# Feed-forward of a hybrid encoder block: nine of eleven chunks with the weights as the stationary operand and the activations moving

## The reference, cut to what matters

```
def rms_norm(x, g):
    y = x * rsqrt(mean(x * x, -1) + 1e-6)
    return y * g
def swiglu(h, w_gate, w_up, w_down):
    return (silu(h @ w_gate) * (h @ w_up)) @ w_down
for l in range(2):
    x = x + 0.5 * swiglu(rms_norm(x, ffn1_norm[l]), ...)     # w_gate, w_up: 1024 x 2816
    x = x + concat([attention, pooling], -1) @ w_out[l]       # mixing, not touched but for banks
    x = x + 0.5 * swiglu(rms_norm(x, ffn2_norm[l]), ...)     # w_down: 2816 x 1024
```

## Time and profile before

| | us |
|---|---|
| median of three runs | 951.69 |
| the profiled execution | 951.97 |
| its span, first to last instruction | 949.9 |
| PE busy | 931.3 |
| PE weight loads (beside the products) | 760.5 |
| DVE busy | 551.5 |
| ACT busy | 499.7 |

### The profile page before, as it was taken

How to read it: one execution, slowest core, us unless ns; L and a number is a source line. 1 busy time by engine, 2 the same in 40 slices (tenths; PEclk the granted TensorE clock), 3 DMA queues, 4 the chain that set the end, 5 groups by cost and what they waited for, 6 DMA issues and landing times.

```text
span 949.9 us, 12733 instructions
## 1 busy us (share of the span) xinstructions
PE 931.3 (98%) x4299; PEld 760.5 (80%) x4299; DVE 551.5 (58%) x896; ACT 499.7 (53%) x821; POOL 44.6 (5%) x81
## 2 busy tenths in 40 slices
PE   8899999999999999999999999999999999999996
PEld 6688888877777888888888888888877888888885
DVE  4546465467755655645476545565686474554644
ACT  6545454456746554545465445454675374554542
POOL 1001010010001100100010000000100000000000
PEclk9999999999999999999999999999999999999999
DMA  7967868726235987675456656644534266465541
GB/s 240 251 202 165 230 175 288 257 90 232 104 110 143 273 183 234 158 222 180 133 189 210 220 182 246 213 157 164 175 139 146 74 237 209 172 210 188 168 142 45
DMA packets 123532, 174.66 MB, mean 184 GB/s; under 512 B 8384, under 2 KB 99696, under 8 KB 123248
## 3 DMA queue, kind: packets, MB, share of 16 engines
q1 hardware_dynamic: 117744, 165.70, 52.0%
q0 software_dynamic: 2848, 6.38, 5.5%
q10 hardware_dynamic: 2912, 2.22, 0.7%
HBM read 173.14 MB, written 4.19 MB: 187 GB/s over the span
## 4 chain that ended last, share of the span: by engine, by line
PE 92%; DVE 3%; ACT 2%; issue 2%; DMA 1%; SPq 0%; POOL 0%; POOLq 0%; DVEq 0%; ACTq 0%
PE ps L985 28%; PE ps L988 28%; PE ps L986 28%; PE ps L1082 2%; PE ps L995 1%; DVE w_lo L727 1%; PE ps L996 1%; PE ps L1195 1%; ACT xt_hi L487 1%; PE ps L1211 1%; PE ps L1223 1%; PE ps L1070 1%; DMA w_raw<-in_ffn_w_down_dram 1%; PE ps L1045 0%; DVE w_lo L718 0%
## 5 line engine op out<-in xcount | busy, mean ns | idle before, releaser
L985 PE MATMUL ps<-w_hi,xt_hi 128*128 128x512 f32 x856 | 342.1, 400 | 2.1 <-DVE xt_lo L741 1.1
L727 DVE SCALAR_TENSOR_TENSOR w_lo<-w_raw,gains,w_hi 128x512 fp32r<-128x512 f32 x416 | 285.1, 745 | 85.8 <-ACT w_hi L472 84.3
L986 PE MATMUL ps<-w_lo,xt_hi 128*128 128x512 f32 x856 | 334.3, 390 | 0.0
L988 PE MATMUL ps<-w_hi,xt_lo 128*128 128x512 f32 x856 | 329.5, 391 | 0.0
L472 ACT ACTIVATE w_hi<-w_raw,gains 128x512 fp32r<-128x512 f32 x408 | 260.7, 713 | 86.2 <-PE ps L988 81.5
L718 DVE TENSOR_TENSOR w_lo<-w_raw,w_hi 128x1024 fp32r<-128x1024 f32 x104 | 122.8, 1222 | 136.1 <-ACT w_hi L465 135.7
L985 PEld LDWEIGHTS ps<-w_hi,xt_hi 128*128 128x128 f32 x856 | 161.2, 188 | 40.3 <-issue 4.0
L988 PEld LDWEIGHTS ps<-w_hi,xt_lo 128*128 128x128 f32 x856 | 161.1, 188 | 34.8
L986 PEld LDWEIGHTS ps<-w_lo,xt_hi 128*128 128x128 f32 x856 | 161.4, 189 | 30.7
L465 ACT ACTIVATE w_hi<-w_raw 128x1024 fp32r<-128x1024 f32 x104 | 104.4, 1052 | 121.7 <-PE ps L988 114.4
L985 PE MATMUL ps<-w_hi,gt_hi 128*128 128x512 f32 x352 | 138.3, 393 | 3.3 <-DVE gt_lo L782 3.3
(11 more groups left out here) (84 smaller groups left out, 404.2 us busy)
## 6 DMA issues: line engine op xcount, KB each, us to landing
w_raw<-in_ffn_w_down_dram SPq DMA_DIRECT2D x88, 512.0 KB, 4.2
w_raw<-in_ffn_w_gate_dram SPq DMA_DIRECT2D x86, 512.0 KB, 4.0
w_raw<-in_ffn_w_up_dram SPq DMA_DIRECT2D x86, 512.0 KB, 5.1
w_raw<-in_w_in_dram SPq DMA_DIRECT2D x32, 512.0 KB, 4.8
w_raw<-in_w_out_dram SPq DMA_DIRECT2D x16, 512.0 KB, 5.3
bias_scratch<-in_rpb_dram POOLq DMA_DIRECT2D x32, 96.0 KB, 8.2
bias<-bias_scratch POOLq DMA_DIRECT2D x2, 1536.0 KB, 6.8
pool_m<-in_pool_matrix_dram ACTq DMA_DIRECT2D x1, 1024.0 KB, 9.3
```

The source lines that it names most:

```text
L727: nc.vector.scalar_tensor_tensor(w_lo[slot][:, part], w_raw[slot][:, part], g, w_hi[slot][:, part].bitcast(F32), ALU.mult, ALU.subtract).t ...
L985: nc.tensor.matmul(o, hi, wh, start=start, stop=False)
L986: nc.tensor.matmul(o, hi, wl, start=False, stop=False)
L988: last = nc.tensor.matmul(o, lo, wh, start=False, stop=bool(stop))
```

## The change

Chunks 0 and 1 of a stage stay as they were. For chunks 2 to 10 the operands of gate and up trade places. The stationary operand is now a 128x128 block of the weights, the moving operand is the normalised, transposed activation `xn`, 256 tokens at once. The output has hidden columns on partitions and tokens along the row, which is the form that the down product wants, so `gated` is not transposed any more. For one chunk there are 2 halves of rows, gate and up, 2 column blocks, 4 row blocks and 3 products: 96 products of 256 columns where there were 48 of 512. They go to banks 0, 1 (gate) and 6, 7 (up).

For that, each stage makes `xn` once while chunk 1 runs: PE spreads `rstd` over a row (`broadcast_rstd`), ACT stores it, DVE multiplies the transposed residual with gain and `rstd` (`normalise_xt`, 8 instructions of 256 columns), ACT and DVE split it (`split_xn_hi`, `split_xn_lo`). The transposed residual must stay in PSUM until then, so `transpose_resid` writes the accumulator banks now, and the first down product waits for `normed_t_ready`. The weights of chunks 2 to 10 are split without the gain, by 2 instructions of 1024 columns where there were 4 of 512. `silu` and `gate_t` work on 512 columns at once. The order of loads in SP's loop changes from g0, g1, d to g0, d, g1.

```diff
-                with sp.Fori(2, N_FF_CHUNKS) as i:
-                    load_gate_up(layer, ff, weights, i, 0)
-                    load_gate_up(layer, ff, weights, i, 1)
-                    load_down(layer, ff, weights, i - 1, ff["d"], i - 1)
+                with sp.Fori(2, LAST) as i:
+                    load_gate_up(layer, ff, weights, i + 1, 0)
+                    load_down(layer, ff, weights, i, ff["d"], i)
+                    load_gate_up(layer, ff, weights, i + 1, 1)
...
+            def silu_t_of(layer, ff, i):
+                act.wait_ge(gate_ready, transposed_no(layer, ff, i) + 1)
+                nc.scalar.activation(silu[:, :, :], ps[:, 0:2, 0:SEQ], ACT.Silu
+                                     ).then_inc(silu_t_ready, 1)
...
+            def gate_t(layer, ff, i, part):
+                dve.wait_ge(up_ready, transposed_no(layer, ff, i) + 1)
+                dve.wait_ge(silu_t_ready, transposed_no(layer, ff, i) + 1)
+                nc.vector.scalar_tensor_tensor(gated[:, :, part], ps[:, 6:8, part], 0.5,
+                                               silu[:, :, part], ALU.mult, ALU.mult
+                                               ).then_inc(gated_t_ready, 1)
...
+            def normalise_xt(layer, ff):
+                dve.wait_ge(rstd_row_stored, ff_no(layer, ff) + 1)
+                for k in range(KT):
+                    h, c = k // 4, (k % 4) * P
+                    done = nc.vector.scalar_tensor_tensor(
+                        normed_t(k).rearrange("p (t q) -> p t q", t=TT),
+                        ps[:, 2 + h:6 + h:2, c:c + P], gains[:, ff["stage"], layer, k:k + 1],
+                        rstd_row[:, :].rearrange("p (t q) -> p t q", t=TT), ALU.mult, ALU.mult)
+                    if k % 4 == 3:
+                        done.then_inc(normed_t_ready, 1)
...
-                        last = nc.tensor.transpose(ps[:, 6 + h, k * P:(k + 1) * P],
+                        last = nc.tensor.transpose(acc(t, h)[:, k * P:(k + 1) * P],
                                                    resid[:, t, c:c + P], ident[:, :])
...
+            def broadcast_rstd(layer, ff):
+                for t in range(TT):
+                    pe.wait_ge(rstd_ready[t], layer * STAGES + (ff["stage"] + 1))
+                    last = nc.tensor.matmul(ps[:, 7, t * P:(t + 1) * P],
+                                            rstd[:, t, :].to_broadcast([P, P]), ident[:, :],
+                                            start=True, stop=True)
+                last.then_inc(rstd_row_ready, 1)
+
+            def gate_up_t(layer, ff, i, a, free_gate=None, free_up=None):
+                slot = ff["g"][a]
+                number = unit_no(layer, ff["stage"], slot, i)
+                for m, free in ((0, free_gate), (1, free_up)):
+                    if free:
+                        pe.wait_ge(*free)
+                    for j in range(2):
+                        out_cols = ps[:, GU_BANKS[m][j], 0:SEQ]
+                        for k in range(4):
+                            if (m, j) == (0, 0):
+                                wait_split(slot, number, k + 1)
+                            c = k * BANK + m * FC + j * P
+                            w_h, w_l = w_hi[slot][:, c:c + P], w_lo[slot][:, c:c + P]
+                            x_h = xn[:, 4 * a + k, 0, :]
+                            x_l = xn[:, 4 * a + k, 1, :]
+                            nc.tensor.matmul(out_cols, w_h, x_h, start=(a, k) == (0, 0), stop=False)
+                            nc.tensor.matmul(out_cols, w_h, x_l, start=False, stop=False)
+                            last = nc.tensor.matmul(out_cols, w_l, x_h, start=False,
+                                                    stop=(a, k) == (1, 3))
...
+                broadcast_rstd(layer, ff)
                 chunk(layer, ff, 1, True)
-                with pe.Fori(2, LAST) as i:
-                    chunk(layer, ff, i, False)
...
+                transpose_gated(layer, ff, 1)
+                pe.wait_ge(xn_lo_ready, 2 * ff_no(layer, ff) + 2)
+                gate_up_t(layer, ff, 2, 0, free_up=(gt_lo_ready, gt_no(layer, ff, 1) + 1))
+                all_down(layer, ff, 1)
+                gate_up_t(layer, ff, 2, 1)
+                with pe.Fori(TOKEN_MAJOR + 1, LAST) as i:
+                    done = transposed_no(layer, ff, i)
+                    gate_up_t(layer, ff, i, 0, (silu_t_ready, done), (gated_t_ready, gated_t_no(layer, ff, i)))
+                    all_down(layer, ff, i - 1)
+                    gate_up_t(layer, ff, i, 1)
```

More of the change, by code:

```diff
@@ L565, in ff_stage @@
                 unit_g1(layer, ff, 1)
[L566 to L572 removed]
+                store_rstd_row(layer, ff)
+                unit_down(layer, ff, 0)
+                store_gt_hi(layer, ff, 0)
+                silu_of(layer, ff, 1, 0)
+                for h in range(2):
+                    split_xn_hi(layer, ff, h)
+                unit_g0(layer, ff, 2, gained=False)
+                silu_of(layer, ff, 1, 1)
+                unit_g1(layer, ff, 2, gained=False)
+                unit_down(layer, ff, 1)
+                store_gt_hi(layer, ff, 1)
+                with act.Fori(TOKEN_MAJOR, LAST) as i:
+                    unit_g0(layer, ff, i + 1, gained=False)
+                    unit_down(layer, ff, i)
+                    silu_t_of(layer, ff, i)
+                    unit_g1(layer, ff, i + 1, gained=False,
+                            used=(up_ready, transposed_no(layer, ff, i) + 1), halves=(0,))
+                    split_gated_hi(layer, ff, i)
+                    unit_g1(layer, ff, i + 1, gained=False, halves=(1,))
                 if ff is FF1:
@@ L794, in unit, with split_xn_lo @@
+            def split_xn_lo(layer, ff, h):
+                dve.wait_ge(xn_hi_ready, 2 * ff_no(layer, ff) + h + 1)
+                nc.vector.tensor_tensor(xn[:, 4 * h:4 * h + 4, 1, :],
+                                        normed[:, h, :].rearrange("p (k q) -> p k q", k=4),
+                                        xn[:, 4 * h:4 * h + 4, 0, :].bitcast(F32), ALU.subtract).then_inc(xn_lo_ready, 1)
+            def unit(layer, ff, slot, k, gains_from=None, halves=(0, 1)):
                 split_lo(slot, unit_no(layer, ff["stage"], slot, k),
-                         gains_of=None if gains_from is None else (ff["stage"], layer, gains_from))
+                         gains_of=None if gains_from is None else (ff["stage"], layer, gains_from),
+                         halves=halves)
@@ L935, in store_gains @@
                     gains[:, first:last, :, :].rearrange("p j l k -> p (j l k)"),
[L936 removed]
+                    ps[:, 5 + n, first * DEPTH * KT:last * DEPTH * KT]).then_inc(gains_stored, 1)
             store_gains(1, 0, 1)
@@ L1129, in chunk, with all_down @@
                         transpose_gated(layer, ff, i - 1)
-                n = unit_no(layer, ff["stage"], d, i - 1)
+                pe.wait_ge(normed_t_ready, 2 * ff_no(layer, ff) + 2)
+                all_down(layer, ff, i - 1, first)
+            def all_down(layer, ff, i, first=False):
+                n = unit_no(layer, ff["stage"], ff["d"], i)
                 for t in range(TT):
                     for k in range(2):
-                        last = down(layer, ff, i - 1, t, k, d, n, t == 0, start=first and k == 0)
+                        last = down(layer, ff, i, t, k, ff["d"], n, t == 0, start=first and k == 0)
                 last.then_inc(down_used, 1)
```

167 lines of the change are left out of this document (101 added, 66 removed).

## The result

| | before | after |
|---|---|---|
| median of the timed runs | 952.02 us (950.94 to 953.25, 4 runs) | 967.12 us (965.98 to 968.05, 4 runs) |
| profiled execution, and its span | 951.97 us, 949.9 us | 966.84 us, 965.0 us |

The changed kernel is slower by a ratio of 1.0156 (95% interval 1.0142 to 1.0169). I had predicted 964 us in a range of 936 to 988. The mechanism was the one I had priced. One term, the wait for a PSUM bank, was twice what I had put.

A forecast was written before the change was run, and what follows sets the result against it. PE was taken to bound the kernel (busy 931.3 of 949.9 us, 92% of the chain). 951.97 + 24.1 (products) - 16.9 (transposes) + 1.6 (rstd) + 3.6 (bank) = 964.4, less 0.3: 964 us, range 936 to 988.

The forecast's parts named there:

- Products: Gate and up, chunks 2 to 10: 96 products of 256 columns at 0.1205 us replace 48 of 512 at 0.227, +24.1 us.
- a fixed loss of 0.014: Each float32r product or its weight load loses 0.014 us over its columns: 0.107 + 0.014 = 0.1205 us; chance 0.48.
- two readings: Product loss fixed (0.1205 us at 256 columns, 964 us, chance 0.48) or proportional to columns (0.1135, 940 us, chance 0.24).
- Transposes: Gated-activation transposes on PE: eight of ten full groups at 0.47 us and two end halves gone per stage, -16.9 us.
- Spreading rstd: Two plain float32 products of 128 columns on PE, taken as 0.4 us a stage, +1.6 us.
- normalising: Normalising and splitting xn on DVE and ACT during chunk 1: covered by 1.1 us before PE wants the weights, nothing lost.
- The bank: Chunk 2's up products wait for `gt_lo` of chunk 1 in bank 7: PE waits 0.9 us a stage, +3.6 us.
- a bound for late weights of chunk 2: In the bank wait: 2 us a stage if the weights of chunk 2 land later than 315.20.
- The loop: From chunk 3 on: no PE wait, ACT and DVE savings worth nothing, chunk pitch 17.0 us instead of 16.82.

The follow-up runs named there:

- Experiments 1 and 2: Kernel before: with 9 probe groups of 24 products behind it (float32r 227, 173, 120 ns); with chunks 2-10's gate/up products halved to 256 columns, 974.87 us.
- experiment 6: Changed kernel, chunk 1's transposed block stored before down unit 1 is split, and second layer's bias rows fetched in the first attention: 959.88 us, 1.0087 to the kernel before.
- Experiment 5: Changed kernel, second layer's bias rows fetched during the first mixing stage's attention, not the second feed-forward stage: 964.46 us, 1.0130 to the kernel before.
- Experiment 4: Changed kernel, ACT and DVE store chunk 1's transposed block before making down unit 1's high and low parts: 965.07 us, 1.0130 to the kernel before.
- experiment 8: Changed kernel, high weights meet [high | low] activations in one product of 512 columns, halves then copied and added: 963.20 us, 1.0131 to the kernel before.

## Why the prediction was right, and where not

- *Products.* 0.1205 was predicted and 0.120 measured, +22.3 us instead of +24.1. I argued from a bound (a fixed loss of 0.014) against the nearest row in plain float32, which loses nothing. That the loss "goes with float32r" was right; that it was fixed was a guess between two readings which no row of the kernel before could tell apart, so there is luck in the 0.1205. Experiments 1 and 2 have since told them apart.
- *Transposes.* -16.9 predicted; 32 groups out of the 36 that this is worth were taken out by themselves and gave -15.3 for a predicted -15.0.
- *Spreading rstd* (+1.6) *and normalising* (nothing). Stages 2 and 3 without any wait are 1.9 us longer than before (experiment 6). (22.3 - 16.9) / 4 = 1.35 of that is products and transposes, so 0.6 is left where I had 0.4. The recorded starts show where: the first down product of stages 2 to 4 comes 25.4 us into the stage instead of 24.9 to 25.0, which is the 0.4 of the spreading, and the other 0.2 lies behind it and stays open. In stage 4 the kernel's end behind the last down product is 0.9 us shorter than before (7.0 for 7.9), so the whole difference there is only 1.0. Why the end is shorter stays open, and so do the 1.2 of stage 1. Normalising is never waited for by PE, as predicted. It did use up 3 us of lead that the load of down unit 1 had (1.7 us for its second DMA), which mattered in stage 2.
- *The bank.* This is the term that was mis-sized: "PE waits 0.9 us", +3.6 in all. It was 6.9, and 1.5 of lower clock behind the longest. The steady value, 1.16 to 1.45, is close. The failed step is "ACT starts their high part when down is through, at 321.5, so DVE is not held by it". In stage 2 ACT started at 326.59, as the weights had not landed; that is 33.1 us into the stage, where 321.5 is 30.9. I had kept a bound for late weights of chunk 2 and none for this unit, and had followed neither its release to the DMA issue (3.0 us later in the stage) nor its landing beside the fetched rows. Experiment 5 leaves the late issue and takes away the fetches, and there ACT again starts as soon as down is through. But "so DVE is not held by it" failed in every stage. DVE was idle for ACT's high part for 1.10 us in stage 1, 1.34 in stage 3, 0.52 in stage 4, and 0.53 in stage 2 of experiment 5. Stage 3 of the changed kernel:
```profile
519.12 2.01 ACT L500 ACTIVATE w_hi<-w_raw 128x1024 fp32r<-128x1024 f32 x2 [3.44 <-PE ps L1097]
520.29 2.36 DVE L784 TENSOR_TENSOR w_lo<-w_raw,w_hi 128x1024 fp32r<-128x1024 f32 x2 [1.34 <-ACT w_hi L500]
```
  DVE was free 31.2 us into this stage, where my sum has 32.1, and then waited for ACT, so the 0.9 came near the measured wait by another path, which is luck.
- *The loop.* Pitch 17.0 predicted, 16.98 measured, no wait in it: right. That ACT and DVE have room said nothing about the transfers. Experiment 4 shows that there the loop has little to spare.

The sum: 22.3 - 16.9 + 1.6 (as predicted) + 6.9 + 1.5 = 15.4, against 965.0 - 949.9 = 15.1 between the spans. The misses (-1.8 in the products, +4.8 in the waits and the clock) partly cancelled, so the 964 is a little better than its parts.

## What to carry to other kernels

Where TensorE is full, count products and not only columns. Read the price of one from start to start, subtract the columns at the clock, and ask whether the rest is per column or per product before making products shorter; a probe of 24 products behind the kernel answers it. When an instruction is put on an engine that frees load buffers, follow the release to the DMA issue and to its landing, and look twice before a short store that frees a bank stands behind a weight split that waits for a load. Removing a wait can change the order in which two streams of transfers meet, so a wait's length is not the gain from its removal.

## What the runs showed of the hardware

- Float32r products with 128 stationary columns are spaced 13 to 14 ns over their columns at 2.4 GHz for 256, 384 and 512 columns (120, 173, 227), and take 112 ns at 128 columns. Bfloat16 loses 2.5 ns and goes down to 56 at 128 columns.
- With 512 and 256 columns in turn, float32r takes 353 ns a pair and not 347, in one bank or two. Bfloat16 takes 325, the sum of its parts.
- A load of up weights of 512 KB took 4.7 us to land (the median) in a stage without fetches of small rows. Issued about 1 us ahead of two such fetches it took 4.8 to 5.5 us, issued 3 to 4 us behind them 9.3 to 11.5. That order is why 18 loads had a median of 5.2 us in one kernel and 11.3 in the other with the same 12 fetches; why the order matters stays open.
- The clock is not foretold by the length of a pause. In the changed kernel 3.26 us without a product's start were followed, 1.1 us after work began again, by 15 products at the 1.2 GHz level. In experiment 8 a pause of 2.7 us (stage 1) was followed by a granted clock of 0.59 as well, and one of 3.7 us (stage 2) was not:
```profile
49.00:53.00 4.00, 3.88 (x13) 3.34 (x14) 0.07 (x1) 0.00 (x0) 0.00 (x0) 0.59 0.82 269
...
331.10:336.00 4.90, 4.86 (x25) 4.16 (x26) 0.51 (x1) 1.68 (x2) 1.48 (x2) 1.00 0.78 264
```
